# Where the weight buffers of a two-block fp32 kernel begin within a 128-byte line

## What is computed

```python
for i in range(2):                      # first block
    m = nsa_mixer(...) if i == 0 else ssd_mixer(...)     # of rms_norm(h)
    h = h + rms_norm(m, gains[1])
    f = conv_ffn(rms_norm(h, gains[2]), ffn_w_up[i], ffn_conv_w[i], ffn_conv_b[i], ffn_w_down[i])
    h = h + rms_norm(f, gains[3])
y = concat([gdn_branch(u @ gdn_w_in), memory_attention(...)]) @ w_out     # second block
h = h + rms_norm_2(y, norm_post_mix)
f = swiglu(rms_norm_2(h, norm_pre_ffn), w_ffn_in, w_ffn_out)
h = h + rms_norm_2(f, norm_post_ffn)
```

## Time and profile before

| | |
|---|---|
| median of three runs | 1207.46 us |
| span of the profiled execution | 1202.5 us |
| PE busy | 1176.9 us (98%) |
| PEld busy | 1076.7 us (90%) |
| DVE busy | 847.2 us (70%) |
| ACT busy | 651.3 us (54%) |
| POOL busy | 151.4 us (13%) |
| read from HBM | 193.09 MB, 161 GB/s over the span |

### The profile page before, as it was taken

How to read it: one execution, slowest core, us unless ns; L and a number is a source line. 1 busy time by engine, 2 the same in 40 slices (tenths; PEclk the granted TensorE clock), 3 DMA queues, 4 the chain that set the end, 5 groups by cost and what they waited for, 6 DMA issues and landing times.

```text
span 1202.5 us, 23183 instructions
## 1 busy us (share of the span) xinstructions
PE 1176.9 (98%) x9852; PEld 1076.7 (90%) x9852; DVE 847.2 (70%) x1299; ACT 651.3 (54%) x1171; POOL 151.4 (13%) x143
## 2 busy tenths in 40 slices
PE   8999999999999999999999999999999999999998
PEld 8897789999889898978999988999989878999986
DVE  6677777888557988886788874857577776655542
ACT  4657556666446665644666653665435534644431
POOL 1320000000002332101000000103443311000000
PEclk9999999999999999999999999999999999999999
DMA  8842225565625443353755564442222322755540
GB/s 308 268 141 89 98 101 207 192 210 194 231 106 176 151 182 141 114 184 105 259 196 181 206 245 158 178 176 106 107 107 71 120 93 92 277 196 190 184 167 35
DMA packets 31622, 196.67 MB, mean 164 GB/s; under 512 B 4000, under 2 KB 5664, under 8 KB 9376
## 3 DMA queue, kind: packets, MB, share of 16 engines
q1 hardware_dynamic: 27504, 185.17, 43.1%
q10 hardware_dynamic: 4016, 10.03, 2.6%
HBM read 193.09 MB, written 1.05 MB: 161 GB/s over the span
## 4 chain that ended last, share of the span: by engine, by line
PE 88%; DVE 5%; ACT 3%; issue 2%; POOL 1%; DMA 0%; DVEq 0%; POOLq 0%; ACTq 0%
PE bank L538 24%; PE bank L540 24%; PE bank L539 24%; DVE wlo L527 2%; PE bank L1894 1%; PE bank L1132 1%; PE bank L1189 1%; PE bank L1216 1%; ACT whi L519 1%; PE bank L725 1%; PE bank L2538 1%; PE bank L3005 1%; PE bank L2481 1%; POOL rr L667 0%; PE bank L2525 0%
## 5 line engine op out<-in xcount | busy, mean ns | idle before, releaser
L527 DVE TENSOR_TENSOR wlo<-raw,whi 128x1024 fp32r<-128x1024 f32 x322 | 389.0, 1245 | 87.9 <-ACT whi L519 87.3
L538 PE MATMUL bank<-xT,wlo 128*128 128x256 f32 x1488 | 418.6, 281 | 4.2 <-DVE wlo L527 2.1
L539 PE MATMUL bank<-xT,whi 128*128 128x256 f32 x1488 | 413.1, 278 | 0.0
L540 PE MATMUL bank<-xT,whi 128*128 128x256 f32 x1488 | 413.1, 278 | 0.0
L519 ACT ACTIVATE whi<-raw 128x1024 fp32r<-128x1024 f32 (+1 forms) x349 | 349.2, 1048 | 115.9 <-PE bank L540 86.7
L538 PEld LDWEIGHTS bank<-xT,wlo 128*128 128x128 f32 x1488 | 279.5, 188 | 7.9 <-DVE xc L1601 2.8
L539 PEld LDWEIGHTS bank<-xT,whi 128*128 128x128 f32 x1488 | 279.6, 188 | 0.6 <-issue 0.5
L540 PEld LDWEIGHTS bank<-xT,whi 128*128 128x128 f32 x1488 | 279.4, 188 | 0.0
L667 POOL TENSOR_TENSOR rr<-rr,nhalf 128x1 f32<-128x1 f32 x34 | 24.7, 729 | 710.0 <-DVE rr L655 522.4
L538 PE MATMUL bank<-whi,gT 128*128 128x512 f32 x264 | 104.6, 396 | 0.0
L540 PE MATMUL bank<-whi,gT 128*128 128x512 f32 x264 | 104.4, 395 | 0.0
(11 more groups left out here) (390 smaller groups left out, 1766.5 us busy)
## 6 DMA issues: line engine op xcount, KB each, us to landing
raw<-in_wall SPq DMA_DIRECT2D x173, 1024.0 KB, 4.8
grow<-in_rows ACTq DMA_DIRECT2D x13, 512.0 KB, 5.3
h<-in_x SPq DMA_DIRECT2D x4, 256.0 KB, 5.3
dsk<-in_rows ACTq DMA_DIRECT2D x4, 256.0 KB, 3.4
memx<-in_mem ACTq DMA_DIRECT2D x1, 1024.0 KB, 10.5
out<-h SPq DMA_DIRECT2D x4, 256.0 KB, 2.0
masks<-in_masks SPq DMA_DIRECT2D x1, 580.0 KB, 13.3
D<-Tx ACTq DMA_DIRECT2D x4, 128.0 KB, 5.8
```

The costliest lines, as they stand in the source:

```text
L527: e.tensor_tensor(low, src, high, SUB).then_inc(*up("dve.low", p))
L538: e.matmul(out, a[1], b[0], start=start, stop=False)
L539: e.matmul(out, a[0], b[1], start=False, stop=False)
L540: return e.matmul(out, a[0], b[0], start=False, stop=stop)
```

## The change

Four tiles of `whi` and four of `wlo`, made one by one, become slices of one tensor each. Slice i begins 2052 x i columns in, that is 8208 x i bytes, which is 16 x i bytes into a 128-byte line. Each tensor is 32 columns (128 bytes) longer than its four tiles were together, so that everything allocated behind them moves by 256 bytes. Nothing else in the program differs; instructions, waits and shapes are the same.

```diff
         raw = [sb([128, 2048], name="raw") for _ in range(NRAW)]
-        whi = [sb([128, 2048], f32r, name="whi") for _ in range(NHL)]
-        wlo = [sb([128, 2048], f32r, name="wlo") for _ in range(NHL)]
+        whi, wlo = ([w[:, 2052 * i:2052 * i + 2048] for i in range(NHL)]
+                    for w in (sb([128, 2048 * NHL + 32], f32r, name=n) for n in ("whi", "wlo")))
         cols = sb([128, _NCOL], name="cols")
```

## The result

The changed kernel takes 1214.4 us (median of four runs, 1213.5 to 1214.4), the kernel before in the same session 1207.5 us (1204.2 to 1207.8). The ratio is 1.0065, with a 95% interval of 1.0042 to 1.0089: slower. The profiled execution took 1214.37 us with a span of 1212.5, so 1.9 us lie outside the span. The span of before is 1202.5, so the profiled one must be the run of 1204.2 us (the other runs leave 1.8 or 1.9 us outside, not 5), and span to span the change costs 10.0 us.

The account below looks back on a forecast made before the run. PE, busy for 98% of the span, bounds the kernel through the time between matmul starts. Terms 6.9 - 1.4 + 0.7 - 0.5 = +5.7 us on 1207.5 gave 1213.2 us, range 1195 to 1222.

Parts of the forecast that it names:

- Base: Whole kernel: forecast starts from the 1207.5 us median, taking 5.0 us beyond the 1202.5 us span as unchanged.
- FFN up projections: Three FFNs, 2736 matmuls at 113.3 ns: three weight buffers of four get slower, +6.9 us on PE's path.
- the straight line from 64 to 0 bytes: Time between 256-column matmul starts: 113.3 ns at 64 bytes, then 115.0, 116.7, 118.3 at 48, 32, 16, and 120.0 at 0.
- Buffer 0 "stays at 0": Weight buffer 0 keeps its place in the line, so only the three other buffers were priced as changing.
- the rival of a broken rhythm: FFN up projections lose the fast rate as places change every 48 matmuls, all at 117.8 ns: +12.3 us, 1221.6 us; chance 0.14.
- Other `xT`-moving ones: 1728 matmuls with `xT` moving outside the FFN stretches, at 117.8 ns: three quarters come to 116.7, -1.4 us.
- `w` moving: 864 matmuls with weights moving and `xT` stationary, taken at 115.6 ns: three quarters get 1.1 ns slower, +0.7 us.
- `mT`: 192 matmuls of `mT` with weights, at 120.0 ns: three quarters come to be 16 to 48 bytes apart, -0.5 us.
- 512 columns: 1128 matmuls with 512 moving columns, at 233.2 ns: taken as 0, bounds -5.6 to +5.8 us.
- ACT and DVE: ACT and DVE accesses to the shifted tiles: nothing; even 5% more, 17 and 19 us, would go into idle time.
- The faster rival: Other distances avoid bank collisions better, slow rates fall to 113.3 ns, FFNs stay: -8.3 us, 1199.2 us; chance 0.32.
- No change: Only halves of a line count, or PE's starting time sets the rate: 1207.5 us; chance 0.20.

Follow-up runs that it names:

- all16: Changed kernel with all eight weight slices at byte 16 of a line, 48 bytes from `xT`: 1214.8 us, ratio 1.0088 to the kernel before.
- all32: Changed kernel with all eight weight slices at byte 32 of a line, 32 bytes from `xT`: 1221.7 us, ratio 1.0146 to the kernel before.
- pack: Changed kernel with every weight slice back at byte 0 of a line, the 128- and 256-byte moves kept: 1200.8 us, ratio 0.9973 to the kernel before.
- shift256: Kernel before with 256 unused bytes behind `wlo`, ahead of `cols`: 1204.1 us, ratio 1.0006.
- all64: Changed kernel with all eight weight slices at byte 64 of a line, 0 bytes from `xT`: 1224.0 us, ratio 1.0164 to the kernel before.
- both16: Kernel before with `whi` and `wlo` in one tensor, weights and `xT` both shifted by 16 bytes, still 64 apart: 1201.5 us, ratio 0.9972.
- xt0: Kernel before with only `xT` moved, to byte 0 of a line, 0 bytes from the weights: 1221.9 us, ratio 1.0141.
- both16b: Kernel before with weights and `xT` shifted 16 bytes, `gT`, `yT`, `yG` 16 bytes ahead of the weights modulo 256: 1199.3 us, ratio 0.9960.

## Why the prediction was right, and where it was wrong

The forecast was 1213.2 us and the result 1214.4, slower as forecast. Its main step held: what the change does is done to the distance between matmul starts, by the distance of the operands in the line, and it is done where the fast rate had been. But the agreement to 1.2 us is partly luck; the terms were off by more, in both directions, and slower had no more than 0.48 of the chances.

- Base. "The 5.0 us between lie outside the span" was wrong. Some 1.9 us lie outside, as for the changed kernel; the other 3 are that the profiled run was one of the lower level and the median one of the upper. Against a run of its own level, 1204.2, the kernel lost 10.2 us, not 6.9. Had I known it and added 5.7, I would have given 1209.9.
- FFN up projections: +6.9 predicted, +10.8 measured. The count was right, the straight line from 64 to 0 bytes was not. `all16` and `all32` have 117.9 and 119.0 for distances of 48 and 32, where the line has 115.0 and 116.7. At a distance of 16 the changed kernel has 118.3 or 115.6, where the line has 118.3. The row that I set aside as "optimistic" to go by, the 118.5 of the earlier trace rows for a tile off its place, was the better guide.
- Buffer 0 "stays at 0" and was priced at nothing. Two of the five chunks in buffer 0 of each FFN's 19 run at 118.7: 2 x 48 x 3 x 5.4 ns = 1.6 us of the 10.8. To this extent the rival of a broken rhythm may have been real, as a side effect in the one buffer that can still be fast; what slows these chunks isn't shown; as the cause of the loss it fell with `all16`, which loses it all without any change of place. Its price, though (113.3 to 117.8 throughout, +12.3), came nearer to the measured term than my own.
- Other `xT`-moving ones: -1.4 predicted, +1.3 measured. The expected gain, slow pairs brought below 117.8, hardly came: the new places have 117.7 to 118.8, with 115.6 in the best case. 1.5 of the +1.3 is a stretch of 16 matmuls 213 ns apart, at 398.3 us, taken up below; without it the term is about 0.
- `w` moving: +0.7 predicted, +1.9 measured. It isn't the stagger: `pack` has the same 104.8 us with all places as before. The old half-and-half of the two rates may be such a choice, which an edit elsewhere can tip; that isn't shown. `mT`: -0.5 predicted, 0 measured.
- 512 columns: 0 predicted, -2.9 measured, inside the bounds of -5.6 to +5.8. The step that failed is "tensors behind `wlo` move by 256 bytes, which leaves their places in a line as they are". It is true of a 128-byte line, and `shift256` shows that a whole 256 bytes do nothing; but `wlo` itself moves by 128, and for 512 columns the place modulo 256 counts. `pack` has -4.7 for this alone, and the stagger takes +1.8 of it back. The count of 1128 left out 96 matmuls with `xT` stationary, which at a price of 0 changed nothing.
- ACT and DVE: nothing predicted, nothing measured, on 349 and 322 instructions. PE's waits were left alone too.
- The faster rival fell: none of the distances tried beats the fast rate that 64 can have. No change fell as well. The Trainium skill (Advanced Engine Details and Errata, Memory Cachelines) has a penalty where each access hits another 16-byte line, by which a shift by whole 16-byte lines costs nothing; `all16` against `pack` is +14 us with the crossings the same, so for this pair of reads the measurement decides against it.

The order of the losses (64 bytes best, the rest 4 to 6 ns worse than its fast rate) is shown by six placements that agree (`pack`, `all16` to `all64`, `both16`, `xt0`), for 48 bytes with the doubt told at `all16`. What in the chip makes it so, no run here shows.

## What to carry to other kernels

In a kernel bound by a stream of matmuls, look at the time between starts, not at durations, and compare it between stretches with the same shape: where it differs by a few per cent, look at the start addresses of the two operands relative to each other, and move either with one line. Changing tile sizes or adding a small tensor ahead of them moves all of that as well, so a change that ought to do nothing can cost 1% or more (`all64` 1.6%) or give a little (`both16b` 0.4%). And where runs of one kernel stand at two levels a few us apart, first find out which level the profile is from.

## What was not expected of the hardware

- At a distance of 64 bytes the same matmuls at the same addresses run 113.4 or 117.9 ns apart for 100 us on end, 4.0 us for an FFN, and choose between the two only after an interruption. At 48, 32 and 0 bytes, with all buffers alike, no up projection was faster than 117.8; at 16, half of the chunks of the changed kernel had 115.6.
- For 512 moving columns the same kind of dependence has a period of 256 bytes: 226.8 ns level, 233.2 at 128 bytes, and `gT` at the same place in a 128-byte line in both.
- The Trainium skill (SBUF — State Buffer, SBUF: two separate sides) says of contention between engines that PE never waits on anyone. What is seen here lies within PE's own stream: 113.4 to 119.2 ns by the placement of its two operands alone. No run tells whether it is the reads that wait.
- The changed kernel's trace has one stretch at the lower clock level, 1.2 GHz, between 398.3 and 401.7 us, right behind a stretch in which PE was half idle. In the rows of the windows (columns as in the windows of the profile after) the granted clock of the second is 0.57, and 16 distances in it are 213 ns each, 1.5 us more than at the full level. In the kernel before, PE is busy for 2.50 of the 4 us from 390 to 394 us, and the granted clock there and in the 4 us behind is 1.00.

```profile
394.00:398.00 4.00, 2.08 (x16) 1.55 (x15) 3.30 (x8) 2.47 (x4) 0.00 (x0) 1.00 0.52 172
398.00:402.00 4.00, 4.00 (x24) 4.00 (x23) 3.97 (x7) 2.67 (x4) 1.19 (x1) 0.57 0.22 90
402.00:406.00 4.00, 4.00 (x37) 4.00 (x36) 3.30 (x7) 1.98 (x5) 1.92 (x1) 1.00 0.71 262
```
